# Cached keys and values between the first attention jobs, the sample one tile later, and the gating sum on VectorE

## The reference

```python
xn = rms_norm(x, g_attn)
q, k, v, qi, ki, wi, u, vs = split(xn @ w_in)      # 512,512,512,512,64,8,512,512 columns
q, k, qi, ki = rope(...)                           # 8 heads x 64
score = einsum('bths,bth->bts', relu(qi . ki), wi) * idx_scale
score = where(allowed, score, -inf)                # chunk-causal, chunks of 64
top_idx = top_k(score, min(256, L // 4))           # per query
attn = softmax(q . k[top_idx] / 8) @ v[top_idx]
vn = layer_norm(gelu(vs)) per group of 128
s = einsum('gij,bcjge->bcige', masked w_s, vn) + b_s   # gating sum with bias
sgu = gelu(u) * s
h = x + concat([attn, sgu]) @ w_out
y = h + (silu(rms_norm(h) @ w_gate) * (rms_norm(h) @ w_up)) @ w_down ; final rms_norm
```

## Time and profile before

| | |
|---|---|
| median of 3 runs | 1463.13 us (1462.37 to 1468.41) |
| the profiled execution | 1470.07 us |
| its span | 1468.1 us |
| mean granted clock of TensorE | 0.947 of full |
| busy share TensorE / VectorE / ScalarE / GpSimd | 88% / 56% / 49% / 30% |

### The profile page before, as it was taken

One profiled execution on the slowest core, in us unless ns is written; L12 is line 12 of the kernel. 1 busy time (PEld: TensorE's weight loads), 2 busy tenths in 40 slices (PEclk: granted clock), 3 DMA queues, 4 the chain that ended last, 5 costly groups with the idle time before them and its releaser, 6 DMA issues.

```text
span 1468.1 us, 29504 instructions
## 1 busy us (share of the span) xinstructions
PE 1288.5 (88%) x10636; PEld 927.3 (63%) x10636; DVE 827.8 (56%) x1512; ACT 717.2 (49%) x1408; POOL 444.4 (30%) x518
## 2 busy tenths in 40 slices
PE   5968887999995347788997999999999998999997
PEld 3443334544443225566454888888888887888887
DVE  4323675789988275997755655555555552212022
ACT  3545788888785524886333544444444442001011
POOL 4772436377279300000202333333333310000001
PEclk9987999999998578999998999999999999999999
DMA  5221000112111200101430222222222128121013
GB/s 192 87 63 32 15 13 34 58 45 79 58 31 31 77 1 16 58 17 59 138 115 29 59 57 57 57 57 57 57 57 57 29 79 212 44 79 37 0 30 90
DMA packets 81596, 86.69 MB, mean 59 GB/s; under 512 B 6768, under 2 KB 63120, under 8 KB 81520
## 3 DMA queue, kind: packets, MB, share of 16 engines
q1 hardware_dynamic: 76112, 75.07, 17.7%
q10 hardware_dynamic: 4848, 8.99, 1.6%
q0 software_dynamic: 560, 1.61, 0.4%
HBM read 72.34 MB, written 13.31 MB: 58 GB/s over the span
## 4 chain that ended last, share of the span: by engine, by line
PE 52%; DVE 8%; ACT 3%; issue 2%; POOL 2%; DMA 2%; SPq 1%; POOLq 0%; DVEq 0%; ACTq 0%
PE PS L1155 28%; PE PS L1212 14%; PE PS L1118 5%; DVE M L1891 2%; DVE M L1880 2%; PE PS L1015 1%; PE PS L1038 1%; PE PS L1068 1%; DMA M<-in_w_down 1%; SPq L647 1%; ACT M L1481 1%; PE PS L1199 1%; ACT M L1492 1%; PE PS L1132 0%; DVE M L1857 0%
## 5 line engine op out<-in xcount | busy, mean ns | idle before, releaser
L1155 PE MATMUL PS<-M 128*128 128x264 f16 x3696 | 420.7, 278 | 9.6 <-ACT M L1600 9.6
L1155 PEld LDWEIGHTS PS<-M 128*128 128x128 f16 x3696 | 363.3, 98 | 66.5 <-ACT M L1600 10.2
L889 PE MATMUL PS<-M 128*128 128x512 f16 (+1 forms) x1512 | 306.9, 364 | 3.6 <-DVE M L441 3.6
L1212 PE MATMUL PS<-M 128*128 128x256 f16 x2112 | 233.5, 274 | 5.9 <-DVE M L2113 5.9
L889 PEld LDWEIGHTS PS<-M 128*128 128x128 f16 (+1 forms) x1512 | 139.5, 103 | 154.2 <-issue 14.2
L1212 PEld LDWEIGHTS PS<-M 128*128 (+1 forms) x2112 | 207.3, 98 | 31.7 <-issue 6.8
L683 POOL TENSOR_TENSOR small<-small 128x1 f32<-128x1 f32 x27 | 5.5, 205 | 520.9 <-ACT M L1547 271.1
L1787 DVE TENSOR_SCALAR_CACHE_REDUCE M<-M,small 128x384 f16<-128x384 f32 (+5 forms) x162 | 132.9, 880 | 0.8
L837 POOL TENSOR_TENSOR M<-M 128x264 f32<-128x264 f32 x44 | 34.8, 791 | 283.1 <-ACT M L1600 283.1
L1952 DVE SCALAR_TENSOR_TENSOR M<-M 128x2048 f16<-128x2048 f32 (+1 forms) x44 | 89.0, 2025 | 36.2 <-ACT M L1538 36.2
L2113 DVE SCALAR_TENSOR_TENSOR M<-PS,M 128x256 f32 (+1 forms) x32 | 13.6, 424 | 165.7 <-PE PS L1212 165.6
(11 more groups left out here) (177 smaller groups left out, 1903.5 us busy)
## 6 DMA issues: line engine op xcount, KB each, us to landing
M<-in_w_in SPq DMA_DIRECT2D x24, 512.0 KB, 3.8
M<-in_w_gate SPq DMA_DIRECT2D x22, 512.0 KB, 4.1
M<-in_w_up SPq DMA_DIRECT2D x22, 512.0 KB, 5.2
M<-in_w_down SPq DMA_DIRECT2D x20, 512.0 KB, 3.9
M<-in_x_prompt SPq DMA_DIRECT2D x16, 512.0 KB, 4.8
M<-in_w_out SPq DMA_DIRECT2D x8, 512.0 KB, 3.8
h_scratch<-M ACTq DMA_DIRECT2D x8, 512.0 KB, 5.0
M<-h_scratch SPq DMA_DIRECT2D x16, 256.0 KB, 7.7
```

The costliest lines, as they stand in the source:

```text
L889: last = pe.matmul(bank(b)[:, 0:w], xnT[:, ds(t, 1), k, s, :].squeeze(1), wt[wbuf(c)][:, k * w:(k + 1) * w], start=(k == 0 and i == 0), st ...
L1155: last = pe.matmul(o, wsp[x][:, zw, wb, k * P:(k + 1) * P], ablk[:, ab, za, k * HT + s * SC:k * HT + (s + 1) * SC], start=(name not in kep ...
L1212: last = pe.matmul(o[:, 0:256], cols[:, ds(m * SC + r * P, P)], wt[dc % 2][:, f, :], start=(f == 0 and i == 0), stop=(f == FT - 1 and i == 2))
```

## The change

- The sample's two packed jobs come after tile 2 instead of after tile 1; the three late masks move from jobs 1, 3, 5 to jobs 2, 6, 10 and use a second pair of scratch buffers (in the unused ends of two logit buffers).
- Cached keys are loaded first, cached values second, all through three slots. The stage of the cached keys and the rounding and subtraction of cached values in the query chunk are gone. The first two key tiles are rounded and subtracted at the end of the query chunk, the others between the jobs: the rounding of tile j+2 in job j (jobs 0 to 13), TensorE's turning of key tile j and its copy in job j (jobs 0 to 7). GpSimd subtracts them one by one after the query chunk.
- The gating sum is taken out by VectorE, in one operation with the bias broadcast: tile 0 ahead of the opening counts of the search, tile b ahead of round b.
- ScalarE's first count of a step moves from behind `E` to behind the roundings.

The core of the diff:

```diff
-ATT_TILES = [0, 1, LAST] + list(range(2, LAST))
+ATT_TILES = [0, 1, 2, LAST] + list(range(3, LAST))
-        tie = [d[:, 0:TOK] for d in dump]
+        tie = [[d[:, 0:TOK] for d in dump], [view(RW, oX + 4608 * i + 1024, [TOK], F16) for i in range(2)]]
         def kc_slot(u):
-            return u % 2 if u < 8 else (u - 8) % 3
+            return u % 3
-        MASK_JOBS = {2 * i + 1: EARLY_MASKS + i for i in range(NS - EARLY_MASKS)}
+        MASK_JOBS = {4 * i + 2: EARLY_MASKS + i for i in range(NS - EARLY_MASKS)}
-                src = a["cache_v" if u < 8 else "cache_k"][0, 0].rearrange("s h d -> s (h d)")
+                src = a["cache_k" if u < 8 else "cache_v"][0, 0].rearrange("s h d -> s (h d)")
@@ gpsimd, step of the projection
-                    if NAMES[c] == "q" and not (isinstance(t, int) and t == 0):
-                        pool.wait_ge(kc_hi, t)
-                        v = Vs[:, ds(t - 1, 1)].squeeze(1)
-                        pool.tensor_tensor(v[:, :, 1, :], heads(kc32[(rep - 1) % 2]), v[:, :, 0, :],
-                                           ALU.subtract).then_inc(kc_lo, 1)
@@ gpsimd, after the projection
+            def cached_low(u):
+                pool.wait_ge(kc_hi, u + 1)
+                v = kchl[u % 2] if u < 8 else Vs[:, u - 8]
+                pool.tensor_tensor(v[:, :, 1, :], heads(kc32[kc_slot(u)]), v[:, :, 0, :],
+                                   ALU.subtract).then_inc(kc_lo, 1)
+            cached_low(0)
+            cached_low(1)
             pool.wait_ge(post_evac, n_unit(NC - 1, LAST) + 2)
...
-            for i in range(8):
-                pool.wait_ge(kc_hi, 8 + i + 1)
-                pool.tensor_tensor(kchl[i % 2][:, :, 1, :], heads(kc32[kc_slot(8 + i)]), kchl[i % 2][:, :, 0, :],
-                                   ALU.subtract).then_inc(kc_lo, 1)
+            for u in range(2, 16):
+                cached_low(u)
@@ tensor
-            for i in range(8):
-                pe.wait_ge(kc_lo, 8 + i + 1)
+            def turn_cached(i):
+                pe.wait_ge(kc_lo, i + 1)
...
             for j in range(NJ):
                 if j + 3 < NJ:
                     qk(j + 3)
+                if j < 8:
+                    turn_cached(j)
@@ scalar, step of the projection
                     E(c, t, rep)
-                    if searching(c, t):
-                        sign_count(c, t, 0)
...
                     lagged(not_vs(H), c, t, rep, 1)
                     lagged(not_vs(ST), c, t, rep, 1)
-                    if NAMES[c] == "u":
-                        sgu_evac(c, t, rep)
+                    if searching(c, t):
+                        sign_count(c, t, 0)
...
                     lagged(R, c, t, rep, 2)
-                    if NAMES[c] == "q" and not (isinstance(t, int) and t == 0):
-                        act.wait_ge(kc_loaded[(rep - 1) % 2], ((t - 1) // 2 + 1) * 16)
-                        act.activation(Vs[:, ds(t - 1, 1), :, 0, :].squeeze(1), heads(kc32[(rep - 1) % 2]),
-                                       ACT.Copy).then_inc(kc_hi, 1)
@@ scalar, after the projection
+                if c == NC - 1:
+                    cached_high(0)
+                    cached_high(1)
...
             for j in range(NJ):
                 if j + 2 < NJ:
                     exp(j + 2)
+                if j < 8:
+                    cached_turned(j)
+                if j + 2 < 16:
+                    cached_high(j + 2)
@@ vector
+            def sgu_evac(t):
+                p = par(cC["u"], t)
+                dve.wait_ge(spatial_done, t + 1)
+                wait_r_free(dve, cC["u"], t, p)
+                dve.scalar_tensor_tensor(out=heads(r32[p], GROUPS), in0=heads(bank(6 + t % 2), GROUPS), scalar=1 / WS,
+                                         in1=bs.unsqueeze(2).broadcast_to([P, GROUPS, P]), op0=ALU.mult,
+                                         op1=ALU.add).then_inc(spatial_evac, 1)
...
             link(dve.memset(cand, 0))
+            dve.wait_ge(ln_loaded, 48)
+            sgu_evac(0)
             for j in range(NS):
                 count(j, n_sel[0] - (j > 0))
...
             for b in range(1, 32):
+                if b < NT:
+                    sgu_evac(b)
                 bit_round(b)
```

More of the change, by code:

```diff
@@ L1320, in dup_q @@
                 act.activation(v[:, :, 1, :], v[:, :, 0, :], ACT.Copy).then_inc(dup_done, 1)
-            def sgu_evac(c, t, rep):
-                p = par(c, rep)
-                act.wait_ge(spatial_done, t + 1)
-                wait_r_free(act, c, t, p)
-                for g in range(GROUPS):
-                    last = act.activation(r32[p][:, g * P:(g + 1) * P], bank(6 + rep % 2)[:, g * P:(g + 1) * P],
-                                          ACT.Identity, scale=1 / WS, bias=bs[:, g:g + 1])
-                last.then_inc(spatial_evac, 1)
             def vs_squares(c, t, rep):
@@ L1403, in score_relus, with cached_high @@
                     head(i * 2 + 1, 1, False)
+            def cached_high(u):
+                act.wait_ge(kc_loaded[kc_slot(u)], 16 * kc_loads(u))
+                if 2 <= u < 8:
+                    act.wait_ge(kc_turned, u - 1)
+                out = kchl[u % 2] if u < 8 else Vs[:, u - 8]
+                act.activation(out[:, :, 0, :], heads(kc32[kc_slot(u)]), ACT.Copy).then_inc(kc_hi, 1)
             def searching(c, t):
@@ L1503, in cached_turned @@
                 act.activation(kTs[:, :, i * P:(i + 1) * P], bank16(1 + 2 * (i % 2)), ACT.Copy).then_inc(kc_evac, 1)
-            for i in range(8):
-                u = 8 + i
-                act.wait_ge(kc_loaded[kc_slot(u)], 16 * kc_loads(u))
-                if i >= 2:
-                    act.wait_ge(kc_turned, i - 1)
-                act.activation(kchl[i % 2][:, :, 0, :], heads(kc32[kc_slot(u)]), ACT.Copy).then_inc(kc_hi, 1)
-                if i:
-                    cached_turned(i - 1)
-            cached_turned(7)
             exp(0)
@@ L1851, in mask @@
                 sc = scores[:, SC_OFF[t]:SC_OFF[t] + S]
-                eq, rank = tie[0][:, 0:S], tie[1][:, 0:S]
+                eq, rank = (x[:, 0:S] for x in tie[j >= EARLY_MASKS])
                 link(dve.tensor_scalar(rank, sc, kth[:, j:j + 1], None, ALU.is_gt, ALU.add,
@@ L1873, in peak @@
                     dve.wait_ge(cmask_ready, 1)
-                if t >= 2:
+                if t == LAST:
                     dve.wait_ge(mask_ready, 1)
```

## The result

The changed kernel takes 1475.20 us in the median of 20 runs (1471.43 to 1478.14). The kernel before, run on the same chip in turn with it, takes 1468.33 us (20 runs, 1462.37 to 1474.14). The ratio is 1.0045, with a 95% interval of 1.0033 to 1.0058: slower by 6.9 us, by less than the 0.5% named in the prediction, but beyond the interval. The forecast of 1463.0 was 12.2 us too low, and 1475.2 lies 0.2 above its range. Of the 12.2, 5.2 come from the median of three runs (1463.13) on which the forecast was laid, and the rest is what the change costs.

The account below looks back on a forecast made before the run. VectorE was taken to pace the small jobs, GpSimd the query chunk, and ScalarE's and VectorE's exchange the gating chunk. -18.1 + 11.8 + 9 - 3.6 + 1 = +0.1, laid on the median 1463.13, gave 1463 us, range 1452 to 1475.

Parts of the forecast that it names:

- Part 1: Between the last query copy and the first logits: the cached keys' own stage goes, -18.1 us.
- Part 2: The 16 small jobs of attention tiles 0 and 1 grow with cached tiles between them, +11.8 us.
- Part 3: Gating chunk and search: the gating sum on VectorE delays the key chunk's first copy, +9 us.
- Part 4: Query chunk: moved sign count gains about 1.0, the subtraction leaving GpSimd 2.6; together -3.6 us.
- Part 5: Attention: new order of tiles moves eight output weight pieces eight jobs later, +1 us.
- A: Rival, gating chunk: the search catches up or its counts aren't held by the first sum; 1449 us, chance 0.20.
- B: Rival, small jobs: the ring of cached tiles runs one tile at a time; +11.4, 1474 us, chance 0.13.
- C: Rival, under the masks: GpSimd and VectorE exclude each other for whole operations; +4.6, 1468 us, chance 0.14.

Follow-up runs that it names:

- g: The changed kernel with the cached key tiles as a block of their own ahead of the jobs, values still between them; 1481.7 us, ratio 1.0099.
- h5: The changed kernel with gating sum on ScalarE, sign counts in their old place and five masks instead of four ahead of the first peak; 1453.0 us.
- k: The kernel before the change with six masks instead of four ahead of the first peak; 1456.7 us, ratio 0.9912.
- b: The kernel before with only the gating sum on VectorE and the sign counts behind the roundings; 1484.1 us, ratio 1.0101.
- c: The changed kernel with the first gating sum moved behind the opening counts and first turned bits; 1467.3 us, ratio 0.9992.
- f: The changed kernel with the old order of attention tiles (0, 1, the sample's, then the rest); 1471.6 us, ratio 1.0032.
- d: The changed kernel with each gating sum behind the counts of a round instead of ahead of them; 1462.3 us, ratio 0.9949.
- e: The changed kernel with the gating sum back on ScalarE, sign counts left behind the roundings; 1459.3 us, ratio 0.9941.
- a: The changed kernel with the gating sum back on ScalarE and the sign counts in their old place; 1459.4 us, ratio 0.9939.
- j: The changed kernel with gating sum on ScalarE, sign counts in their old place, six early masks and the old tile order; 1448.0 us, ratio 0.9868.

## Why the prediction was right or wrong

**Part 1, right.** -18.1 given, -18.0 measured, with the last query copy directly in front of the table load. g adds that the block was dear because nothing of it was prepared: with two tiles ready it takes 13.1.

**Part 2, right in its mechanism, met in size with some luck.** +11.8 given. 539.93 in the earlier trace rows is the low part of job 12, not 15, as the peaks run three jobs ahead. Like for like, low part 12 moved from 38.8 to 49.5 us behind the first logits, +10.7. The new length of 50.7 was counted to low part 15, which stands at 53.1 (548.77), so it was 2.4 too short and was set against a place three jobs too early; the two errors nearly cancel. (50.7 less 38.8 is also 11.9, not 11.8.) A job of tile 0 takes 1.96 to 1.98 us (2.0 given), and the masks grew by 2.2 us together (2.3 given). h5 to k bear out that VectorE sets the pace here.

**Part 3, the step that failed.** The mechanism was right and its places were met within 0.2 us: opening counts 243.8 (243.9), turned bits 251.5 (251.7), second sum 258.6 (258.8), round 1 over at 263.9 (264.1). What failed is "Rounds 2 to 8 cost 5.3 each and four of them a weight piece more (1.22): 42". They cost 47.4 (from 263.89 to 311.33, the ends of the turning). The nine small operations that met GpSimd in these seven rounds took 8.4 us instead of 2.1, which is 6.3 more; all else took 0.9 less than I had put down. VectorE has hardly a wait in them, so what its operations take more goes straight into the length, and neither of the others would have held it up: ScalarE waits 2.0 to 2.3 us for the turned bits in each of these rounds, and TensorE's last gating sum was over at 304.19, 4.0 us before ScalarE copied it. How much 42 asked for is seen in the kernel before, where the same seven rounds run between these two lines:

```profile
246.29 1.19 DVE L1799 SCALAR_TENSOR_TENSOR small<-small 128x7 uint32<-128x7 uint32 x1
...
295.09 0.23 DVE L1799 SCALAR_TENSOR_TENSOR small<-small 128x7 uint32<-128x7 uint32 x1
```

That is 47.8 us from end to end, there with VectorE waiting for ScalarE. So 42 meant that the search catches up by 5.8 us, and it caught up by 0.4. I had allowed for one meeting and written a bound of +13 "if half of the rounds meet GpSimd"; all seven did. That the outcome (+13.6) lies so near this bound is luck: it priced half of the rounds at 4.4 us, and all seven cost 6.3. Everything after that runs as written (5.4 us from the turned bits to the key chunk, 5.7 given), so the first copy came 13.6 us late and not 8.6. A second, smaller error is "the key chunk is held by the ring of main sums": it also starts with TensorE idle and at the lower clock, +1.9.

Why all seven and not half? GpSimd's pair of operations starts when ScalarE has copied the main sum and rounded, and ScalarE does this behind its counts, which start at the turned bits. So both engines' work hangs on the same event, once per round, and a meeting in one round tends to come again in the next. That it repeats is shown: in b, c, f and g the same nine operations take the same times within 0.01 us, though c is done with round 1 10.9 us before b. It doesn't hold for every round: rounds 1 and 9 of the changed kernel meet nothing, nor does one of the first eight of d. That the common event is why, I only argue from the releasers.

**Part 4, right in size, wrong in its split.** -3.6 given, -3.0 measured. The moved count was to bring 1.0, but e and b show no gain (+1.4 and -0.3); so it is the subtraction that brought 3 us or more, where I had 2.6. In a, with the count in its old place, the stretch from the value chunk to the logits is 4.5 us shorter than the same stretch of before up to the last query copy (119.8 against 124.3).

**Part 5, not contradicted.** +1 given; +1.3 in the window behind low part 12 (150.0 against 148.7), nothing to 3 by f and j.

**The rivals.** A (the search catches up) is refuted: VectorE has 0.9 us of waits left from 258 to 312, and only with the sum back on ScalarE does the key chunk begin before 303 (c and d begin it at 306.3 and 307.1). B (the ring serial in the jobs) is refuted by 1.98 us per job, where it needed 3.2. C has the mechanism right and the place wrong: exclusion for whole operations is what the rows show, but it costs 2.2 us under the masks, not 6.9, and 6.3 in the search. The end on the slower side lay in neither, but in a bound of part 3 that I did not follow up.

## What to carry to other kernels

Before an operation goes to another engine, find what it waits for and put it behind whatever doesn't need it: the same 0.69 us operation costs 1.06% ahead of the counts and 0.1 to 0.2% behind them (ratios and medians of a and d, not clear of their intervals). When work on two engines is released by the same event, don't price their meetings by a share of the rounds: work out the distance for one round, since it can come back in the next ones, as it did here in seven running. And before a stage is rebuilt, look for idle time of the pacing engine in front of it: one number moved two masks and brought 0.9% (k).

## What was not expected of the hardware

A VectorE operation on 7 numbers per partition (0.23 us) waits out a GpSimd operation on 512, up to 1.07 us in all, and ends 0.02 to 0.03 us behind it, in nine cases of nine in seven rounds. VectorE's counts on 384 to 896 columns, most of its work there, kept their durations in the same stretch. Under a mask it is the same. GpSimd's timeline has

```profile
503.78 1.23 POOL L809 TENSOR_TENSOR M<-M 128x512 f16<-128x512 f32 x1 [0.82 <-ACT M L1403]
...
518.34 1.65 POOL L809 TENSOR_TENSOR M<-M 128x512 f16<-128x512 f32 x1 [0.93 <-ACT M L1403]
...
532.78 1.15 POOL L809 TENSOR_TENSOR M<-M 128x512 f16<-128x512 f32 x1 [1.06 <-ACT M L1403]
```

and VectorE's scan that started at 504.22, inside the first, took 2.67 us where it took 2.02 before. The product that started at 532.81 took 1.69 instead of 0.77. The second went the other way: GpSimd came 0.11 us after VectorE had begun an operation of 0.75, and took 1.65 instead of 1.15; the scan that VectorE began under it then took 2.93 instead of 2.29. So what a meeting costs is what is left of the operation that began first, less 0.1 to 0.2 us (0.98 left and 0.77 lost at 268.86, 0.79 and 0.65 at 504.22, 0.64 and 0.50 at 518.34), and it depends on which operations meet. The Trainium skill, "SBUF — State Buffer", section "SBUF: two separate sides", states this rule for a GpSimd operation that reads SBUF and a VectorE operation that has two SBUF inputs or runs in a two-port mode: whichever of the two starts first gets the shared pair of ports for the whole instruction, and the other fully blocks. The trace agrees, in the ends that lie 0.02 to 0.03 us apart, and the prediction, which doubted it because both engines were slowed, was too quick to do so.
